# Requesting the first expert's down matrix inside the routing stage

## What is computed

```
tokens = modulate(x, norm_ffn[i], mod[3], mod[4])      # layer 0: 1024 + 256 tokens, layer 1: 1024
g      = top-1 of 4 groups;  e1, e2 = top-2 of the 8 experts in that group
y      = w_1 * expert(e1) + w_2 * expert(e2)
expert(e) = (silu(xs @ w1[e]) * (xs @ w3[e])) @ w2[e]  # w1, w3: 1024 x 512, w2: 512 x 1024
x      = x + mod[5] * y
```

## Time and profile before

| | us |
|---|---|
| median of 3 executions | 2528.12 |
| lowest, highest | 2525.13, 2528.15 |
| the profiled execution | 2529.12 |
| its span, first to last instruction | 2527.3 |
| TensorE busy (products) | 2221.6, 88% |
| VectorE, ScalarE, GpSimd busy | 745.6, 607.3, 182.2 |

### The profile page before, as it was taken

One profiled execution on the slowest core, in us unless ns is written; L12 is line 12 of the kernel. 1 busy time (PEld: TensorE's weight loads), 2 busy tenths in 40 slices (PEclk: granted clock), 3 DMA queues, 4 the chain that ended last, 5 costly groups with the idle time before them and its releaser, 6 DMA issues. The chain is left out here.

```text
span 2527.3 us, 34982 instructions
## 1 busy us (share of the span) xinstructions
PE 2221.6 (88%) x15176; PEld 1058.0 (42%) x15176; DVE 745.6 (30%) x1167; ACT 607.3 (24%) x960; POOL 182.2 (7%) x126
## 2 busy tenths in 40 slices
PE   4799998979996799999999639998996999988874
PEld 3588875544464233333333224443443333332222
DVE  3423226651116011111111173664325111110104
ACT  4421105541114111111111124564103111111111
POOL 0000000000000000000000121352000000000002
PEclk7799999989998899999999859999997999999996
DMA  8201107046543889889999440001006999999995
GB/s 310 64 26 34 42 18 324 1 125 236 205 167 142 365 359 413 350 347 411 415 415 419 135 150 17 25 25 53 22 3 246 419 413 414 413 425 412 428 427 216
DMA packets 139500, 595.84 MB, mean 236 GB/s; under 512 B 25332, under 2 KB 52688, under 8 KB 114640
## 3 DMA queue, kind: packets, MB, share of 16 engines
q1 hardware_dynamic: 109232, 515.42, 51.2%
q0 software_dynamic: 11952, 43.52, 4.7%
q10 hardware_dynamic: 18160, 34.61, 3.7%
HBM read 534.79 MB, written 58.72 MB: 235 GB/s over the span
## 5 line engine op out<-in xcount | busy, mean ns | idle before, releaser
L1743 PE MATMUL ph<-w,x_t 128*32 128x512 f32 x6016 | 680.5, 605 | 41.8 <-DMA w<-in_exp_w 39.6
L1743 PEld LDWEIGHTS ph<-w,x_t 128*32 128x32 f32 x6016 | 190.8, 111 | 454.1 <-issue 429.6
L1756 PE MATMUL py<-w,g_t 128*32 128x512 f32 x3008 | 341.1, 594 | 1.0 <-DVE g_t L1862 1.0
L1856 DVE TENSOR_TENSOR hidden<-hidden,ph 64x512 f32<-64x512 f32 x94 | 102.4, 1089 | 757.5 <-ACT hidden L1814 757.5
L1245 PE MATMUL z<-Y,w_o 128*128 128x512 f32 (+1 forms) x640 | 256.9, 558 | 0.2
L1814 ACT ACTIVATE hidden<-ph 64x512 f32<-64x512 f32 x94 | 55.5, 590 | 696.8 <-PE ph L1743 696.8
L2068 PE MATMUL z<-hT,w_cd 128*128 128x512 f32 (+1 forms) x448 | 184.1, 569 | 4.9 <-ACT hT L490 4.9
L1756 PEld LDWEIGHTS py<-w,g_t 128*32 128x32 f32 x3008 | 93.6, 110 | 205.0 <-issue 203.7
L706 PE MATMUL z<-h_high,w_hi 128*128 128x512 f32 (+1 forms) x432 | 161.5, 374 | 15.3 <-DVE h_low L538 15.3
L1721 POOL DMA_INDIRECT x_rows<-h_tokens,index x47 | 44.3, 943 | 1800.3 <-PE px L1728 982.6
L1245 PEld LDWEIGHTS z<-Y,w_o 128*128 128x128 f32 x640 | 121.1, 193 | 120.5 <-issue 115.2
(11 more groups left out here) (310 smaller groups left out, 2078.7 us busy)
## 6 DMA issues: line engine op xcount, KB each, us to landing
w<-in_exp_w SPq DMA_DIRECT2D x192, 2048.0 KB, 14.4
ada_raw<-in_ada_w SPq DMA_DIRECT2D x24, 2048.0 KB, 8.0
y_slots<-y_rows ACTq DMA_DIRECT2D x188, 128.0 KB, 8.9
y_slots<-zero SPq DMA_DIRECT2D x29, 512.0 KB, 14.7
h_tokens<-h_rows ACTq DMA_DIRECT2D x18, 512.0 KB, 3.0
w_ab<-in_w_in_ab SPq DMA_DIRECT2D x14, 512.0 KB, 3.9
w_cd<-in_w_in_cd SPq DMA_DIRECT2D x12, 512.0 KB, 3.9
x_t_saved<-xT SPq DMA_DIRECT2D x8, 640.0 KB, 8.6
```

The source lines that it names most:

```text
L1743: ins = pe.matmul(ph[row:row + UNIT, :], xt[:, k, at:at + UNIT], w13[place[2 * b + n] % RING][:, half, k, :], start=(k == 0), stop=(k == K ...
L1756: ins = pe.matmul(py[b % 2][row:row + UNIT, :], gt[:, k, n * UNIT:(n + 1) * UNIT], w2[place[2 * b + n] % RING][:, k, half * 512:(half + 1) ...
L1856: dve.tensor_tensor(hid[PAIR:P, :].rearrange("s (k q) -> s q k", k=FT), hid[0:PAIR, :].rearrange("s (q k) -> s q k", k=FT), ph[PAIR:P, :]. ...
```

## The change

In the routing stage SyncE now also requests the down matrix of place 0, directly behind the up and gate matrices of place 0 and ahead of its wait for the stores. The request behind the first gather is dropped; the loop over places 1 to 31 is as it was.

```diff
@@ route, SyncE
                 sp.wait_ge(s_table, 1)
                 first = self.expert_of(sp, 0)
                 self.load_up(sp, layer, ring, 0, first)
+                self.load_down(sp, layer, ring, 0, first)
                 for i in range(HROWS):
                     sp.wait_ge(s_hw[i], 16 * len(range(i, nt, HROWS)))
@@ experts, SyncE
                 sp.wait_ge(s_x, 16)
-                self.load_down(sp, layer, ring, 0, self.expert_of(sp, 0))
                 for j in range(1, NE):
                     e = self.expert_of(sp, j)
```

## The result

The changed kernel took 2540.92 us (median of 5, 2535.31 to 2541.98) against 2528.12 us (median of 5, 2525.13 to 2532.74) for the kernel before: a ratio of 1.0041, interval 1.0028 to 1.0053, that is +10.4 us (7.1 to 13.4). The ratio is estimated from all executions and is not the quotient of the two medians, which lie 12.8 us apart; both differences are inside the interval. A second set of runs of the same two kernels gave 1.0037 (1.0025 to 1.0049). The forecast was +6.3 us: the right sign, and a little under the interval. Its range ended at 2538.5 us: 10.4 us above the kernel before is just that, and the median itself, 2540.92, lies above it.

What follows compares the result with a forecast made beforehand. The prediction took the last store's landing to bound layer 0's seam and VectorE, ending last, layer 1's. Its terms, -1.0 + 4.7 + 2.6 = +6.3 us, gave a median of 2534.4 us, range 2528.5 to 2538.5.

Steps and rivals of the forecast that it cites:

- What bounds the seams: Between routing and expert stages: layer 0 waits for the last store's landing; in layer 1 VectorE ends last.
- The stores' price: Layer 0: the down matrix's bytes delay the last store and so TensorE's start, +4.7 us, bounds 3.9 to 5.1.
- The gather's price: Layer 1: the down matrix's remaining bytes delay the first gather's landing, +2.6 us, bounds 0 to 6.3.
- The direct gain: Layer 0: matrices 1 and 2 land sooner relative to the gather, removing TensorE's 1.0 us wait for weights, -1.0 us.
- The lead does not live on: Layer 1: the 5 us lead of the weights is gone by 1992, so the late waits gain 0.
- a sign against itself: Layer 1: late waits for weights shrinking by 5 us would show the prediction wrong.
- the clock: After each seam: a moved start lengthens or shortens TensorE's half-speed stretches by chance, ±1.5 us a layer, mean 0.
- The early request: Rival, both seams: stores and gathers slip through free and the 1.0 us wait goes, 2527.1 us; chance 0.08.
- One price only: Rival: only layer 1's gather is delayed, +1.6 us, or only layer 0's stores, +3.7 us; chance 0.17.
- The gather in full: Rival, layer 1: the first gather waits as the second does, 6.3 us more; whole change +10.0 us; chance 0.08.

Runs made afterwards that it cites:

- early in layer 0 alone: Changed against the kernel before: down matrix 0 requested early in layer 0 only, layer 1 as before; ratio 1.0028, +7.1 us.
- delay: Kernel before plus two GpSimd products of 128 x 1024 ahead of layer 0's first gather, no DMA added; ratio 1.0020, +5.1 us.
- half delay: Kernel before plus one GpSimd product of 128 x 1024 ahead of layer 0's first gather; ratio 0.9996, -1.0 us.
- changed, again: The changed kernel run a second time, nothing further altered, against the kernel before; ratio 1.0037, +9.4 us.
- early in layer 1 alone: Changed against the kernel before: down matrix 0 requested early in layer 1 only, layer 0 as before; ratio 1.0010, +2.5 us.
- behind the stores: Against the kernel before: down matrix 0 requested in the routing stage of both layers, but after SyncE's wait for the stores; ratio 1.0038, +9.6 us.
- all behind stores: Kernel before with up and gate of place 0 requested after SyncE's wait for the stores, down matrix after the first gather; ratio 0.9999, -0.3 us.
- gate behind stores: Kernel before with only the gate matrix of place 0 requested after SyncE's wait for the stores; ratio 0.9991, -2.3 us.

## Why the prediction was right in kind and short in size

**What bounds the seams** held: layer 0's by the last store, layer 1's by VectorE and the gather.

**The stores' price** was put at 4.7 between 3.9 and 5.1; the start of TensorE moved by 4.9 us, and by 4.5 and 4.6 us in the traces of the other two kernels with the request at that place in layer 0. The even packet counts of the earlier trace rows, carried over to the stretch behind 820, were the right reading. **The gather's price** was put at 2.6; it is 2.9, 2.9 and 3.1. Why no more: the gather could lose no more than what was left of the matrix. In the changed kernel the matrix was nearly out by 1944 and landed at 1946.87, the gather 0.9 us later, at 1947.79.

**The direct gain** of 1.0 us came (1.1), but not from the step named. The late start with its slower first pairs removes that wait without any early request; the term has two possible causes, and the late start alone suffices.

**The lead does not live on**, as forecast. The waits for weights in layer 1 went from 38.6 to 33.6 us in the first profile, which the prediction had named as a sign against itself. But the time from first to last hidden activation did not shrink, and the same stretch of the changed kernel once more had 36.5. Over the eight traces it does not follow the change:

| layer 1, first to last hidden activation | us |
|---|---|
| layer 1 as before: before, early in layer 0 alone, delay, half delay | 516.5, 519.0, 519.3, 516.4 |
| layer 1 changed: changed, again, early in layer 1 alone, behind the stores | 518.9, 516.9, 516.7, 516.1 |

In the first trace of the changed kernel TensorE waited less for weights and was slower itself: from 1960.8 to 2479.8 the granted clock was 0.95 and its products were busy for 483.7 us, against 0.97 and 476.1 us before, from 1953.7 to 2470.1. So the wait that vanished there was no gain. That is one trace; the changed kernel again had 0.97.

**The term that fell short** is the clock, "±1.5 us a layer, with mean 0". It was the right thing to name and the wrong mean. Layer 0, times behind VectorE's end, from the traces (the clock's rise is where the granted clock of the first products goes to 1.00):

| kernel | TensorE starts | clock rises | second low stretch | last hidden activation |
|---|---|---|---|---|
| all behind stores | 7.1 | 15.1 | yes | 601.0 |
| gate behind stores | 7.4 | 15.0 | no | 600.1 |
| early in layer 1 alone | 8.9 | 15.0 | no | 601.0 |
| before | 8.9 | 14.9 | no | 601.2 |
| half delay | 11.1 | 18.4 | no | 603.5 |
| behind the stores | 12.8 | 21.6 | yes | 607.2 |
| early in layer 0 alone | 13.4 | 21.9 | yes | 607.7 |
| changed, again | 13.5 | 21.8 | yes | 607.5 |
| delay | 13.8 | 21.8 | yes | 607.7 |
| changed | 13.9 | 21.8 | yes | 607.8 |

In these traces the rise falls on a few places, and which one it is goes with the start; five late starts out of five had the worst. The second low stretch goes with it less strictly, as it also came with the earliest start of all. So the change pays +1.0 and +1.7 us in layer 0 in both of its traces, 2.7 us in all. In layer 1 it pays nothing: the rise comes 3.2 us later (17.2 us behind VectorE's end instead of 14.0), about as much as the start, and the second low stretch was there before. The prediction took the rise for chance; it is not: it is the same within 0.1 us in both traces of the changed kernel in layer 0, and in all four traces in which layer 1 is as before. With it the sum is 4.9 + 2.9 + 2.7 - 1.1 = 9.4 us, which the two measurements, 10.4 (7.1 to 13.4) and 9.4 (6.3 to 12.4), bear out. The forecast's 6.3 lacks the 2.7.

**The rivals.** The early request was neither free nor a gain: the measured price was +10 us, since the transfer shared its engines with two others that TensorE waits for. The Trainium skill (DMA: Bandwidth & Descriptors, Rules for kernel authors) advises to issue a DMA early; at this seam that did not pay. "One price only" is out: the two kernels with one layer each show both. "The gather in full" had the time nearest to the measured one, +10.0 us, and the time alone would not have ruled it out; the trace does, by the gather's landing in 7.4 us instead of the 10.8 that this rival needs.

## What to carry to other kernels

A matrix that already arrives 11 us early has nothing to gain from an earlier request, and its bytes have to pass whatever is in flight at the new place. List the small transfers that end a stage or open the next one, and give each the added bytes as a delay, engine by engine, as long as the queues alternate. Then add what the delay does to TensorE's clock: a start that comes a few microseconds later can push the rise to the next place.

## What was not expected of the hardware

- Small transfers behind large ones: a store of 512 KB lands in 2.8 us alone, in 8.9 us with 2 MB in flight on another queue, in 14.4 us with 4 MB, in 19.3 us with 6 MB.
- In the ten traces of layer 0 tabled above, the granted clock's rise came at three places against the program's own events: 14.9 to 15.1, 18.4, and 21.6 to 21.9 us behind VectorE's end. A delay of 2.1 us cost 2.2 us, one of 4.9 us cost 6.5.
- With 40 added transposes ahead of a run of small products, TensorE stood 1.3 to 4.8 us at "issue" within it, in each of three traces. That it waited for instructions fits the traces and is not tested.
